# Rotary logits of a latent-KV attention as two single-pass split products in place of one float32 product

## The chip, the cores and the metric

One core of a Trainium2 chip runs the whole program, two transformer blocks for 512 tokens of width 1024. The metric is the device time in microseconds of one execution. Engines are named as the profile names them: PE (TensorE, matmuls), PEld (its weight loads), DVE (VectorE), ACT (ScalarE), POOL (GpSimd) and SP (the queue that issues most loads).

## The reference

The second block's last attention is the one that the change touches. Cut to what matters:

```python
def mla_attention(h, pos, w_dq, cq_norm, w_uq, q_nope_norm, q_pe_norm, w_o, k_nope, k_pe, v):
    c_q = rms_norm_2(h @ w_dq, cq_norm)
    q = (c_q @ w_uq).reshape(b, s, MLA_HEADS, MLA_QK_NOPE + MLA_QK_ROPE)   # 16 heads, 128 + 64
    q_nope = rms_norm_2(q[..., :MLA_QK_NOPE], q_nope_norm)
    q_pe = rotary(rms_norm_2(q[..., MLA_QK_NOPE:], q_pe_norm), pos)
    def block(args):                                                       # 4 blocks of 128 queries
        i, qn, qp = args
        sc = (jnp.einsum('bqhd,bkhd->bhqk', qn, k_nope)
              + jnp.einsum('bqhr,bkr->bhqk', qp, k_pe)).astype(jnp.float32) * scale
        sc = jnp.where(causal_mask(i, s), sc, NEG_INF)
        a = jax.nn.softmax(sc, axis=-1)
        return jnp.einsum('bhqk,bkhv->bqhv', a.astype(v.dtype), v)
```

Each head's logits are a product over 128 plain dimensions and one over 64 rotary dimensions. The rotary keys `k_pe` are shared by all heads.

## The kernel before

Everything is held transposed, features on the 128 partitions and the 512 tokens along the free dimension. The kernel is written as stages, each with one function per engine (`tensor`, `scalar`, `vector`); every engine runs its list of instructions in the order written, and semaphores tie the lists together. Large weight products are made of three passes of float32r data (`mm3`, L317 to L319): the weights and the activations are split into a rounded part and its rest (`w_hi`, `w_lo` by L291 and L300 on DVE), and high by high, high by low and low by high are added up in PSUM. The attention's own products (logits, transposes, values) are float32 matmuls; each of these shows as two instructions in the trace.

The stage `Latents` makes the compressed keys and queries and the rotary keys: `rotary_keys` (L2759 to L2769) leaves `kpe`, which has two versions: the keys in partitions 0 to 63 with zeros below, and the keys in 64 to 127 with zeros above. The zeros are two memsets at the start of the stage's `vector` (L2718, L2719).

The stage `Mla` follows. Its 16 heads are taken as 8 pairs, r from 0 to 7. One tile `qpe` holds both heads' rotary queries of a pair, head 0 in partitions 0 to 63 and head 1 in 64 to 127. A unit u is one head and one block b of 128 queries, so there are 8 units to a pair and 64 in all; block b has 128(b+1) keys. PE's list for unit u is: `logits(u)` (L3406 plain, L3407 rotary, L3408 the causal mask, bf16), the sums of squares (L3385) of what the unit before projected, the projections of the next pair (`mm3` passes or L3335 to L3337), `turn(u-2)` (transposes, L3416), `values(u-3)` (L3430). The projections are spread over units by the tables `EVEN` and `ODD`; `rotate` (L3392) turns the next pair's rotary queries into PSUM bank 7 at the end of unit 4 for an odd r and of unit 6 for an even r.

On DVE unit u is: `row_max(u)` (L3573), `normalize(u-1)` (L3579, L3582), at some units `output_lo` (L3588), `norm_out` of what was projected before (L3559), `round_both` of a weight slot (L291, L300), and last, at the same unit as `rotate`, `rope(r)` (L3562 to L3568): three instructions that end with the rotated queries in `qpe`. ACT has `exp(u)` (L3507), the norm's logarithm and exponential (L3495, L3499), the squares (L3479) and `turned_out` (L3515), which takes the transposed probabilities to `mpt`.

Three waits of PE look at `rope`: the sum of squares of K1 or Q1 waits for its first instruction (it frees bank 7), the first unit of a pair waits for its last, and so does, in `vector`, all that stands behind it on DVE.

Of the kernel before, what the change touches and what calls it, by code (L numbers as in the profile page):

```python
# [20 lines left out]
F32 = mybir.dt.float32  # L21
# [133 lines left out]
class Kernel:  # L155


    def __init__(self, nc, ctx, dram, V):
# [5 lines left out]
        def overlay(*groups):  # L164
# [4 lines left out]
            for n in [n for n in range(len(groups)) if n != widest] + [widest]:  # L169
# [43 lines left out]
            (self.cqh, self.cql, self.ckh, self.ckl, self.cos, self.sin, self.kpe, self.qpe, self.mq, self.mk,  # L213
# [37 lines left out]
             ("cos", [P, T], F32), ("sin", [P, T], F32), ("kpe", [P, 2, T], F32), ("qpe", [P, 2, T], F32),  # L251
# [11 lines left out]
        )  # L263
        self.ps = ctx.enter_context(nc.psum_tensor("ps", [P, 8, T], F32))
# [2254 lines left out]
class Latents(Stage):  # L2519
# [8 lines left out]
    def plan(self):  # L2528
        k = self.k
        self.w = k.slots(self.SIZES, 1)  # L2530
        self.e = k.events(1, gained_hi=range(2 * KD), gained_lo=range(2 * KD), square_summed=[0], log_ms=[0], rstd=[0],
                          evacuated=range(7), norm_sq=range(7), norm_sum=range(3), norm_log=range(3), norm_rstd=range(3),
                          scaled=range(6), x_hi=range(6), x_lo=range(6), norm_out=range(7), rope_rot=[0],
                          rope_step=range(19))
        self.positions_here = k.moved("positions_in")
        self.steps = 0
# [179 lines left out]
    def vector(self, dve):  # L2716
        k, V = self.k, self.k.V
        dve.memset(k.kpe[64:P, 0, :], 0.0).then_inc(k.sem["norm_out"], 1)  # L2718
        dve.memset(k.kpe[0:64, 1, :], 0.0).then_inc(k.sem["norm_out"], 1)  # L2719
# [39 lines left out]
    def rotary_keys(self, dve):  # L2759

        k = self.k
        plain = k.latk[:, 2, :]
        dve.wait_ge(*self.on("rope_step", 18))
        dve.tensor_tensor(k.sq[1][:], k.ps[:, 0, :], k.sin[:], ALU.mult).then_inc(k.sem["norm_out"], 1)
        dve.tensor_tensor(plain, plain, k.cos[:], ALU.mult).then_inc(k.sem["norm_out"], 1)
        dve.wait_ge(*self.on("norm_out", 4))
        for j in range(2):
            own = slice(64 * j, 64 * j + 64)
            dve.tensor_tensor(k.kpe[own, j, :], plain[own, :], k.sq[1][own, :], ALU.add).then_inc(k.sem["norm_out"], 1)  # L2769
# [476 lines left out]
class Mla(Stage):  # L3246
# [10 lines left out]
    ROT_UNIT = {True: 6, False: 4}  # L3257

# [4 lines left out]
    def plan(self):  # L3263
# [3 lines left out]
        for r in range(1, self.PAIRS):  # L3267
# [7 lines left out]
                     if key[1] == "V3" or key[1] == ("K1" if key[0] else "Q1")}  # L3275
# [4 lines left out]
                          rope_made=range(3 * self.PAIRS), logits=u, row_min=u, probs_raw=u, row_recip=u, probs=u,  # L3280
# [95 lines left out]
    def sum_squares(self, pe, r, name):  # L3376
# [4 lines left out]
        if name == {0: "K1", 1: "Q1"}[r % 2] and r:  # L3381
            pe.wait_ge(*self.on("rope_made", 3 * r))
# [5 lines left out]
    def rotate(self, pe, r, after):  # L3388
        k = self.k
        pe.wait_ge(*self.on("norm_out", self.normed[(r, "PE")]))  # L3390
        pe.wait_ge(*self.on("norm_log", self.normed[(r, after)]))
        pe.matmul(k.ps[:, 7, :], k.rot, k.qpe[:, r % 2, :], start=True, stop=True).then_inc(k.sem["rope_rot"], 1)  # L3392

    def logits(self, pe, u):
        k, r, j, b = self.k, u // 8, u // 4 % 2, u % 4
        if b == 0:
            pe.wait_ge(*self.on("norm_out", self.normed[(r, f"Q{j}")]))
            pe.wait_ge(*self.on("norm_out", self.normed[(r, f"K{j}")]))
            if j == 0:
                pe.wait_ge(*self.on("rope_made", 3 * r + 2))  # L3400
# [6 lines left out]
        pe.matmul(bank[:, 0:n], k.qpe[:, r % 2, b * P:n], k.kpe[:, j, 0:n], start=False, stop=False)  # L3407
# [146 lines left out]
    def norm_out(self, dve, r, name):  # L3554
        k, n, V = self.k, self.normed[(r, name)], self.k.V
        dst = k.qpe[:, r % 2, :] if name == "PE" else (k.mq if name[0] == "Q" else k.mk)[:, r % 2, int(name[1]), :]
# [5 lines left out]
    def rope(self, dve, r):  # L3562
        k, own = self.k, self.k.qpe[:, r % 2, :]
# [3 lines left out]
        dve.wait_ge(*self.on("rope_made", 3 * r + 1))  # L3567
        dve.tensor_tensor(own, own, k.rope[:], ALU.add).then_inc(k.sem["rope_made"], 1)  # L3568

# [436 lines left out]
```

## Time and profile before

| what | before |
|---|---|
| median of 3 runs (lowest to highest) | 3025.54 us (3025.52 to 3026.2) |
| profiled execution: span, first to last instruction | 3022.4 us |
| PE busy | 2902.0 us (96%) |
| DVE busy | 1803.7 us (60%) |
| ACT busy | 903.8 us (30%) |
| chain that ended last | PE 87%, DVE 7%, ACT 3%, issue 2% |
| mean granted clock of PE | 0.987 |
| DMA queues in the profile | two "hardware_dynamic", two "instruction" |

The profile gives no time of its own for the profiled execution beside its span; the median of the three runs is 3.1 us above it. The busy share of PE is a sum over matmuls whose ends are modelled, so it hides short stalls. What a stretch is worth has to be read from the chain of waits and from the order of instructions in time.

### The profile page before, as it was taken

The numbers are of one execution on the slowest core, as the hardware profiler recorded it, in microseconds if no ns is written. First come the engines' busy times: TensorE is split into PE (matmuls) and PEld (weight loads), VectorE is DVE, ScalarE is ACT, GpSimd is POOL, SyncE is SP. The second block draws the span as 40 slices with busy tenths as digits, with TensorE's granted clock in tenths as the row PEclk, the third lists the DMA queues.
The fourth block names the chain that finished last, engine by engine and source line by source line (L and its number), as shares of the span: only waits on it lengthen the run. The fifth ranks groups of instructions, "written<-read, shape, count | busy, mean of one in ns | idle before, by whom it ended". The sixth has DMA issues, their size and how long they took to land.

```text
span 3022.4 us, 36545 instructions
## 1 busy us (share of the span) xinstructions
PE 2902.0 (96%) x12794; PEld 2213.6 (73%) x12802; DVE 1803.7 (60%) x2790; ACT 903.8 (30%) x1606; POOL 294.4 (10%) x213
## 2 busy tenths in 40 slices
PE   8999989998998999998999899999889999999999
PEld 6777867776676888866766688887657768788887
DVE  6775356885445555356466777746655554777646
ACT  2111023343433111033255333302355540333202
POOL 1111003332140111000000011100000000011100
PEclk9999999999999999999999999999999999999999
DMA  4335322121122223322221222332211102222332
GB/s 150 109 109 122 104 75 79 63 70 56 49 78 70 90 97 94 96 68 87 86 77 66 77 90 97 97 93 82 87 42 36 36 29 91 82 92 97 97 93 96
DMA packets 78549, 249.86 MB, mean 83 GB/s; under 512 B 8840, under 2 KB 15368, under 8 KB 78440
## 3 DMA queue, kind: packets, MB, share of 16 engines
q1 hardware_dynamic: 65232, 229.74, 23.1%
q10 hardware_dynamic: 13208, 18.71, 2.4%
q8 instruction: 64, 1.05, 0.1%
q14 instruction: 45, 0.37, 0.0%
HBM read 238.32 MB, written 9.96 MB: 82 GB/s over the span
## 4 chain that ended last, share of the span: by engine, by line
PE 87%; DVE 7%; ACT 3%; issue 2%; DMA 0%; ACTq 0%; POOL 0%; SPq 0%; DVEq 0%; POOLq 0%
PE ps L317 24%; PE ps L318 24%; PE ps L319 24%; PE ps L3385 1%; PE ps L3430 1%; PE ps L3406 1%; PE ps L3407 1%; PE ps L906 1%; PE ps L2902 1%; DVE w_lo L300 1%; PE ps L2178 1%; DVE w_hi L291 1%; PE ps L2887 1%; PE ps L2157 1%; PE ps L1545 1%
## 5 line engine op out<-in xcount | busy, mean ns | idle before, releaser
L317 PE MATMUL ps<-xh,w_hi 128*128 128x512 f32 x2152 | 881.2, 409 | 40.6 <-DVE xl L487 13.3
L318 PE MATMUL ps<-xl,w_hi 128*128 128x512 f32 x2152 | 855.7, 398 | 0.0
L319 PE MATMUL ps<-xh,w_lo 128*128 128x512 f32 x2152 | 855.3, 397 | 0.0
L291 DVE CAST w_hi<-raw 128x1024 fp32r<-128x1024 f32 (+1 forms) x438 | 302.5, 691 | 736.2 <-PE ps L319 700.5
L317 PEld LDWEIGHTS ps<-xh,w_hi 128*128 128x128 f32 x2152 | 407.1, 189 | 185.4 <-issue 54.0
L300 DVE TENSOR_TENSOR w_lo<-raw,w_hi 128x1024 fp32r<-128x1024 f32 (+1 forms) x386 | 502.5, 1302 | 28.5
L319 PEld LDWEIGHTS ps<-xh,w_lo 128*128 128x128 f32 x2152 | 406.8, 189 | 100.0
L318 PEld LDWEIGHTS ps<-xl,w_hi 128*128 128x128 f32 x2152 | 407.9, 190 | 98.4 <-issue 7.2
L317 PE MATMUL ps<-ah,w_hi 128*128 128x512 f32 x704 | 278.1, 395 | 0.0
L318 PE MATMUL ps<-al,w_hi 128*128 128x512 f32 x704 | 278.1, 395 | 0.0
L319 PE MATMUL ps<-ah,w_lo 128*128 128x512 f32 x704 | 278.1, 395 | 0.0
L1104 POOL TENSOR_TENSOR al<-tmp,ah 128x512 f32 x44 | 65.0, 1478 | 1353.2 <-ACT ah L1079 1353.2
L310 POOL TENSOR_TENSOR w_lo<-raw,w_hi 128x512 fp32r<-128x512 f32 x104 | 146.8, 1432 | 444.6 <-DVE w_hi L291 444.6
L318 PEld LDWEIGHTS ps<-al,w_hi 128*128 128x128 f32 x704 | 132.0, 187 | 32.4
L317 PEld LDWEIGHTS ps<-ah,w_hi 128*128 128x128 f32 x704 | 132.0, 187 | 32.3
L319 PEld LDWEIGHTS ps<-ah,w_lo 128*128 128x128 f32 x704 | 131.9, 187 | 32.2
L1089 DVE SCALAR_TENSOR_TENSOR tmp<-ps,vecs,tmp 128x511 f32<-128x511 f32 (+1 forms) x176 | 131.1, 745 | 13.7 <-ACT tmp L1074 0.9
L1074 ACT ACTIVATE tmp<-ps,vecs 128x512 f32<-128x512 f32 x88 | 68.6, 780 | 181.1 <-PE ps L319 179.6
L850 POOL TENSOR_TENSOR al<-tmp,ah 128x512 f32 x44 | 57.5, 1306 | 534.4 <-ACT ah L790 534.4
L790 ACT ACTIVATE ah<-tmp 128x512 f32 (+1 forms) x44 | 27.9, 633 | 234.1 <-DVE tmp L828 234.1
L577 ACT ACTIVATE sq<-ps 128x512 f32<-128x512 f32 x24 | 14.4, 599 | 248.4 <-PE ps L319 248.4
L577 ACT ACTIVATE sq<-h 128x512 f32<-128x512 f32 x16 | 10.1, 632 | 218.8 <-DVE h L594 218.8
(429 smaller groups left out, 3707.8 us busy)
## 6 DMA issues: line engine op xcount, KB each, us to landing
raw<-in_ffn_up SPq DMA_DIRECT2D x90, 512.0 KB, 3.3
raw<-in_conv_up SPq DMA_DIRECT2D x88, 512.0 KB, 3.2
raw<-in_ffn_down SPq DMA_DIRECT2D x32, 512.0 KB, 3.6
raw<-in_conv_down SPq DMA_DIRECT2D x32, 512.0 KB, 3.5
raw<-in_merge SPq DMA_DIRECT2D x24, 512.0 KB, 3.2
raw<-in_ple_gate SPq DMA_DIRECT2D x24, 512.0 KB, 3.2
raw<-in_diff SPq DMA_DIRECT2D x24, 512.0 KB, 3.3
raw<-in_mla SPq DMA_DIRECT2D x20, 512.0 KB, 3.2
```

The costliest lines, as they stand in the source:

```text
L291: dve.tensor_copy(self.w_hi[s][:, 0:n], self.raw[r][:, 0:n]).then_inc(self.sem["slot_hi"], 1)
L300: dve.tensor_tensor(self.w_lo[s][:, 0:n], self.raw[r][:, 0:n], self.w_hi[s][:, 0:n].bitcast(F32), ALU.subtract).then_inc(self.sem["slot_sp ...
L310: ins = pool.tensor_tensor(self.w_lo[s][:, own], self.raw[r][:, own], self.w_hi[s][:, own].bitcast(F32), ALU.subtract)
L317: pe.matmul(out, wh, xh, start=start, stop=False)
L318: pe.matmul(out, wh, xl, start=False, stop=False)
L319: return pe.matmul(out, wl, xh, start=False, stop=stop)
L850: pool.tensor_tensor(k.al[:, 2 * i + pair, :], k.tmp[2 * pair][:], k.ah[:, 2 * i + pair, :].bitcast(F32), ALU.subtract).then_inc(k.sem["ac ...
L906: mm = pe.matmul(k.ps[32 * g:32 * g + 32, 4 + r, 0:n], k.bdiag[:], self.selected(b, g), start=True, stop=True)
L1074: act.activation(k.tmp[pos][:], k.ps[:, pos, :], ACT.Identity, bias=self.col(i, pos, 3), scale=self.col(i, pos, 2)).then_inc(k.sem["conv0" ...
L1089: dve.scalar_tensor_tensor(k.tmp[pos][:, back:T], k.ps[:, pos, 0:T - back], self.col(i, pos, 2 - back), k.tmp[pos][:, back:T], ALU.mult, A ...
L1104: pool.tensor_tensor(k.al[:, 2 * i + pair, :], k.tmp[2 * pair][:], k.ah[:, 2 * i + pair, :].bitcast(F32), ALU.subtract).then_inc(k.sem["ac ...
L1545: mm = pe.matmul(k.ps[:, 4 + l % 2, own], keys[:, own], queries[:, own], start=True, stop=True)
```

## The change

The rotary product is no longer one float32 matmul. The rotated queries of a head are split into a rounded part and its rest, both float32r, and stacked: for head 0 the rounded part in partitions 0 to 63 and the rest in 64 to 127, for head 1 the other way round (`qst`, two versions for consecutive pairs). The keys are held three times (`kst`): version 0 is the rounded keys in all 128 partitions, versions 1 and 2 are the rest of the keys in the half where that head's rounded queries lie, and zero in the other. Two float32r matmuls with the same stationary operand then give rounded by rounded plus rest by rounded, and rounded by rest. `rope` gets four more DVE instructions, each of 64 partitions by 512: two rounding copies and two subtractions, the latter writing to the other half of the partitions. `rotary_keys` gets two more. The zeros come from two copies of a constant in place of two memsets. `qpe` has one version in place of two. The new tile `qst` needs room, for which the scratch reserved for dynamic DMA descriptors is set to 8192 bytes.

```diff
-             ("cos", [P, T], F32), ("sin", [P, T], F32), ("kpe", [P, 2, T], F32), ("qpe", [P, 2, T], F32),
+             ("cos", [P, T], F32), ("sin", [P, T], F32), ("kst", [P, 3, T], R), ("qpe", [P, T], F32),
...
+        self.qst = sb("qst", [P, 2, 2, T], F32R)
...
     def vector(self, dve):
         k, V = self.k, self.k.V
-        dve.memset(k.kpe[64:P, 0, :], 0.0).then_inc(k.sem["norm_out"], 1)
-        dve.memset(k.kpe[0:64, 1, :], 0.0).then_inc(k.sem["norm_out"], 1)
+        for j in range(2):
+            rest = slice(64 - 64 * j, P - 64 * j)
+            none = k.half_ones[rest, 64 * j:64 * j + 64].unsqueeze(1).to_broadcast([64, T // 64, 64])
+            dve.tensor_copy(k.kst[rest, 1 + j, :].rearrange("p (a c) -> p a c", c=64), none
+                            ).then_inc(k.sem["norm_out"], 1)
...
         dve.wait_ge(*self.on("norm_out", 4))
+        dve.tensor_tensor(plain, plain, k.sq[1][:], ALU.add).then_inc(k.sem["norm_out"], 1)
+        dve.wait_ge(*self.on("norm_out", 5))
+        dve.tensor_copy(k.kst[:, 0, :], plain).then_inc(k.sem["norm_out"], 1)
+        dve.wait_ge(*self.on("norm_out", 6))
         for j in range(2):
             own = slice(64 * j, 64 * j + 64)
-            dve.tensor_tensor(k.kpe[own, j, :], plain[own, :], k.sq[1][own, :], ALU.add).then_inc(k.sem["norm_out"], 1)
+            dve.tensor_tensor(k.kst[own, 1 + j, :], plain[own, :], k.kst[own, 0, :].bitcast(F32), ALU.subtract
+                              ).then_inc(k.sem["norm_out"], 1)
...
             if j == 0:
-                pe.wait_ge(*self.on("rope_made", 3 * r + 2))
+                pe.wait_ge(*self.on("rope_made", self.ROPE * (r + 1) - 1))
...
         pe.matmul(bank[:, 0:n], k.mq[:, r % 2, j, b * P:n], k.mk[:, r % 2, j, 0:n], start=True, stop=False)
-        pe.matmul(bank[:, 0:n], k.qpe[:, r % 2, b * P:n], k.kpe[:, j, 0:n], start=False, stop=False)
+        rotary = k.qst[:, r % 2, j, b * P:n]
+        pe.matmul(bank[:, 0:n], rotary, k.kst[:, 0, 0:n], start=False, stop=False)
+        pe.matmul(bank[:, 0:n], rotary, k.kst[:, 1 + j, 0:n], start=False, stop=False)
...
     def rope(self, dve, r):
-        k, own = self.k, self.k.qpe[:, r % 2, :]
+        k, own, at = self.k, self.k.qpe[:], self.ROPE * r
...
-        dve.wait_ge(*self.on("rope_made", 3 * r + 1))
+        dve.wait_ge(*self.on("rope_made", at + 1))
         dve.tensor_tensor(own, own, k.rope[:], ALU.add).then_inc(k.sem["rope_made"], 1)
+        dve.wait_ge(*self.on("rope_made", at + 2))
+        head = [slice(64 * j, 64 * j + 64) for j in range(2)]
+        for j in range(2):
+            dve.tensor_copy(k.qst[head[j], r % 2, j, :], k.qpe[head[j], :]).then_inc(k.sem["rope_made"], 1)
+        for j in range(2):
+            dve.wait_ge(*self.on("rope_made", at + 3 + j))
+            dve.tensor_tensor(k.qst[head[1 - j], r % 2, j, :], k.qpe[head[j], :], k.qst[head[j], r % 2, j, :].bitcast(F32),
+                              ALU.subtract).then_inc(k.sem["rope_made"], 1)
...
-    nc = bacc.Bacc("TRN2", target_bir_lowering=False, num_devices=1)
+    nc = bacc.Bacc("TRN2", target_bir_lowering=False, num_devices=1, dynamic_dma_scratch_size=8192)
```

Two places show where the new instructions stand. Line numbers of the changed kernel are its own. The first place is DVE at the rope of pair 3, at unit 4 of pair 2. Before:

```order
L3582 TENSOR_SCALAR sq<-sq,small 128x512 [waits row_recip]
L3565 TENSOR_TENSOR rope<-ps,sin 128x512 [waits rope_rot]
L3566 TENSOR_TENSOR qpe<-qpe,cos 128x512
L3568 TENSOR_TENSOR qpe<-qpe,rope 128x512 [waits rope_made]
L3573 TENSOR_REDUCE small<-ps 128x1 [waits logits]
```

The same place in the changed kernel:

```order
L3602 TENSOR_SCALAR sq<-sq,small 128x512 [waits row_recip]
L3577 TENSOR_TENSOR rope<-ps,sin 128x512 [waits rope_rot]
L3578 TENSOR_TENSOR qpe<-qpe,cos 128x512
L3580 TENSOR_TENSOR qpe<-qpe,rope 128x512 [waits rope_made]
L3584 CAST qst<-qpe 64x512 [waits rope_made]
L3584 CAST qst<-qpe 64x512
L3587 TENSOR_TENSOR qst<-qpe,qst 64x512 [waits rope_made] x2
L3593 TENSOR_REDUCE small<-ps 128x1 [waits logits]
```

Two rounding copies and two subtractions now stand between the end of the rotation and the next unit's `row_max`.

The second place is PE at the end of pair 3, where the sum of squares of K1, a turn, a product with the values and the first logits of pair 4 follow each other. Before:

```order
L3406 MATMUL ps<-mk,mq 128x512 [waits probs_raw]
L3407 MATMUL ps<-kpe,qpe 128x512
L3408 MATMUL ps<-maskc 128x128
L3385 MATMUL ps<-tmp,consts 128x512 [waits rope_made,norm_log,norm_sq]
L3416 MATMUL ps<-consts,rs 128x128 [waits probs_t_out,probs]
L3416 MATMUL ps<-consts,rs 128x128
L3430 MATMUL ps<-mpt,mvr 128x128 [waits y_lo,probs_t_out]
L3406 MATMUL ps<-mk,mq 128x128 [waits rope_made,probs_raw,norm_out]
L3407 MATMUL ps<-kpe,qpe 128x128
L3408 MATMUL ps<-maskc 128x128
```

The same place in the changed kernel:

```order
L3416 MATMUL ps<-mk,mq 128x512 [waits probs_raw]
L3418 MATMUL ps<-kst,qst 128x512
L3419 MATMUL ps<-kst,qst 128x512
L3420 MATMUL ps<-maskc 128x128
L3395 MATMUL ps<-tmp,consts 128x512 [waits rope_made,norm_log,norm_sq]
L3428 MATMUL ps<-consts,rs 128x128 [waits probs_t_out,probs]
L3428 MATMUL ps<-consts,rs 128x128
L3442 MATMUL ps<-mpt,mvr 128x128 [waits y_lo,probs_t_out]
L3416 MATMUL ps<-mk,mq 128x128 [waits rope_made,probs_raw,norm_out]
L3418 MATMUL ps<-kst,qst 128x128
L3419 MATMUL ps<-kst,qst 128x128
L3420 MATMUL ps<-maskc 128x128
```

The order is unchanged but for one rotary matmul that is now two; the wait for `rope_made` at the first logits of a pair now stands for the last of seven rope instructions, not the last of three.

## Rows read from the trace of the kernel before

**Rows 1.** Stretches: us, PE, PEld, DVE, ACT, POOL busy (x), PEclk, DMA share, GB/s

```profile
2196.20:2240.50 44.30, 36.67 (x136) 24.05 (x135) 22.08 (x37) 24.92 (x46) 0.00 (x0) 0.92 0.14 48
2312.40:2384.20 71.80, 71.39 (x345) 51.23 (x345) 37.44 (x78) 37.90 (x86) 0.00 (x0) 1.00 0.11 37
```

**Rows 2.** Chain that ended last, PE's steps in one head: start us, us, what

```profile
2322.93 0.22 PE ps L3407 x2
...
2323.21 0.29 PE ps L3335
2323.49 0.23 PE ps L3336
...
2327.26 0.43 PE ps L3407 x2
...
2332.36 0.65 PE ps L3407 x2
...
2337.76 0.86 PE ps L3407 x2
```

**Rows 3.** Chain that ended last, from the rotation for pair 3

```profile
2312.42 0.69 DVE rope L3565
...
2314.44 0.34 DVE small L3573
...
2319.35 0.48 DVE small L3573
...
2321.67 0.27 ACT mpt L3515
...
2322.07 0.41 PE ps L3416 x2
```

**Rows 4.** Order in time, DVE in the rope of pair 3: start us, us, what [idle before]

```profile
2313.03 0.68 DVE L3566 TENSOR_TENSOR qpe<-qpe,cos 128x512 f32<-128x512 f32 x1
2313.74 0.69 DVE L3568 TENSOR_TENSOR qpe<-qpe,rope 128x512 f32<-128x512 f32 x1
2314.36 0.42 DVE L3573 TENSOR_REDUCE small<-ps 128x1 f32<-128x256 f32 x1
```

**Rows 5.** Order in time, DVE: nearest shapes to the new instructions

```profile
2141.77 0.43 DVE L291 CAST w_hi<-raw 128x512 fp32r<-128x512 f32 x1 [2.59 <-PE ps L319]
...
2199.70 1.41 DVE L2769 TENSOR_TENSOR kpe<-latk,sq 64x512 f32<-64x512 f32 x2
```

**Rows 6.** Order in time, DVE at the ropes of pairs 0 and 4

```profile
2220.59 0.69 DVE L3568 TENSOR_TENSOR qpe<-qpe,rope 128x512 f32<-128x512 f32 x1
2222.72 0.75 DVE L3559 SCALAR_TENSOR_TENSOR mq<-ps,vecs,tmp 128x512 f32<-128x512 f32 x1 [1.43 <-ACT tmp L3499]
...
2360.39 0.69 DVE L3568 TENSOR_TENSOR qpe<-qpe,rope 128x512 f32<-128x512 f32 x1
```

**Rows 7.** Order in time, PE at the first logits of pairs 0 and 4

```profile
2221.43 0.46 PE L3406 MATMUL ps<-mk,mq 128*128 128x128 f32 x2 [0.23 <-DVE qpe L3568]
...
2359.90 1.10 PE L3385 MATMUL ps<-tmp,consts 128*128 128x512 f32 x2
2360.83 0.38 PE L3416 MATMUL ps<-consts,rs 128*128 128x128 f32 x2
2361.05 0.39 PE L3430 MATMUL ps<-mpt,mvr 128*128 128x128 f32 x2
2361.34 0.46 PE L3406 MATMUL ps<-mk,mq 128*128 128x128 f32 x2
```

**Rows 8.** Order in time, PE at waits for the turned probabilities, last pair

```profile
2477.11 0.52 PE L3416 MATMUL ps<-consts,sq 128*128 128x128 f32 x3 [1.01 <-ACT mpt L3515]
```

**Rows 9.** Order in time, DVE behind the zeros and behind the rotary keys

```profile
2132.45 5.40 DVE L2702 SCALAR_TENSOR_TENSOR xl<-h,vecs,xh 128x512 fp32r<-128x512 f32 x8 [1.44 <-ACT xh L2610]
...
2205.76 0.75 DVE L3559 SCALAR_TENSOR_TENSOR mk<-ps,vecs,tmp 128x512 f32<-128x512 f32 x1 [4.65 <-ACT tmp L3499]
```

**Rows 10.** Order in time, PE after idle times elsewhere in the program

```profile
1339.30 0.50 PE L317 MATMUL ps<-xh,w_hi 128*128 128x512 f32 x1 [2.97 <-DVE xl L1330]
...
1340.50 0.63 PE L318 MATMUL ps<-xl,w_hi 128*128 128x512 f32 x1
...
1645.45 0.52 PE L2915 MATMUL ps<-consts,dw 128*128 128x128 f32 x3 [2.80 <-ACT dpt L2998]
```

More of the change, by code:

```diff
@@ L212, in __init__ @@
             (self.oh, self.ol, self.dq, self.dk, self.dvr, self.de, self.dw, self.dpt, self.dout, self.dbias),
-            (self.cqh, self.cql, self.ckh, self.ckl, self.cos, self.sin, self.kpe, self.qpe, self.mq, self.mk,
+            (self.cqh, self.cql, self.ckh, self.ckl, self.cos, self.sin, self.kst, self.qpe, self.mq, self.mk,
              self.mvr, self.mpt, self.rope, self.zh, self.zl),
@@ L2532, in plan @@
                           evacuated=range(7), norm_sq=range(7), norm_sum=range(3), norm_log=range(3), norm_rstd=range(3),
-                          scaled=range(6), x_hi=range(6), x_lo=range(6), norm_out=range(7), rope_rot=[0],
+                          scaled=range(6), x_hi=range(6), x_lo=range(6), norm_out=range(9), rope_rot=[0],
                           rope_step=range(19))
@@ L3257 @@
     ROT_UNIT = {True: 6, False: 4}
+    ROPE = 7
     def __init__(self, k, latents):
@@ L3279, in plan @@
                           norm_out=five, v_out=range(len(values)), rope_rot=range(self.PAIRS),
-                          rope_made=range(3 * self.PAIRS), logits=u, row_min=u, probs_raw=u, row_recip=u, probs=u,
+                          rope_made=range(self.ROPE * self.PAIRS), logits=u, row_min=u, probs_raw=u, row_recip=u, probs=u,
                           probs_t=u, probs_t_out=u, pv=u, y_hi=range(16), y_lo=range(16))
@@ L3381, in sum_squares @@
         if name == {0: "K1", 1: "Q1"}[r % 2] and r:
-            pe.wait_ge(*self.on("rope_made", 3 * r))
+            pe.wait_ge(*self.on("rope_made", self.ROPE * r))
         if (r, name) == (0, "Q1"):
@@ L3391, in rotate @@
         pe.wait_ge(*self.on("norm_log", self.normed[(r, after)]))
-        pe.matmul(k.ps[:, 7, :], k.rot, k.qpe[:, r % 2, :], start=True, stop=True).then_inc(k.sem["rope_rot"], 1)
+        pe.matmul(k.ps[:, 7, :], k.rot, k.qpe[:], start=True, stop=True).then_inc(k.sem["rope_rot"], 1)
     def logits(self, pe, u):
@@ L3555, in norm_out @@
         k, n, V = self.k, self.normed[(r, name)], self.k.V
-        dst = k.qpe[:, r % 2, :] if name == "PE" else (k.mq if name[0] == "Q" else k.mk)[:, r % 2, int(name[1]), :]
+        dst = k.qpe[:] if name == "PE" else (k.mq if name[0] == "Q" else k.mk)[:, r % 2, int(name[1]), :]
         gain = V["b_q_pe_norm" if name == "PE" else "b_q_nope_norm" if name[0] == "Q" else "k_nope_norm"]
```

## The prediction

> **What bounds the kernel now.** I first read the stretches of the last attention. In a period of two pairs of heads PE is busy 71.39 of 71.80 us, DVE 37.44 and ACT 37.90; only the start of the stage, before the second rope, has real holes, 36.67 of 44.30 us [rows 1]. By shares, PE is the bound and DVE is half idle, so PE's savings should count and DVE's additions be free. Busy shares are averages, so I read the chain next. It runs through PE almost everywhere, but at each rope of an odd pair it leaves PE when the rotation is done (2312.42) and comes back only at 2322.07: rope on DVE, the next unit's row maximum, its exponential and the norm on ACT, the weight rounding and another row maximum on DVE, the probabilities' way to `mpt`, then PE's transposes [rows 3]. In those 9.65 us PE works almost the whole time too, and is stopped for a few tenths only: two paths of nearly the same length. Last I read the order in time at the rope of an even pair. There PE's first logits of the new pair start at 2361.34; the product with the values before them began at 2361.05 and takes 0.22, so PE could have started at 2361.27. The rope's last instruction began at 2360.39 and took 0.69, so it ended at 2361.08 [rows 6, 7]. At pair 0 the same wait shows 0.15 from the rope's end (2220.59 + 0.69 = 2221.28) to PE's start at 2221.43. So the even rope is on time to within 0.1 us. There is no slack under `rope` anywhere, and the change makes `rope` longer.
>
> **The change, what PE gains.** The old rotary product takes PE 0.86, 0.65, 0.43 and 0.22 us for 512, 384, 256 and 128 keys [rows 2], 2.16 us for a head. A single-pass float32r matmul of 512 columns takes 0.23 [rows 2], and one that follows another kind takes up to 0.06 more (0.29 against 0.23); the first rotary matmul now follows a float32 one, so I charge 0.05 a unit. No row shows a float32r matmul narrower than 512. I scale the part above 0.02 with the width: 0.18, 0.13 and about 0.08 for 384, 256 and 128. The gains are then 0.86 - 0.47 - 0.05 = 0.34, 0.65 - 0.36 - 0.05 = 0.24, 0.43 - 0.25 - 0.05 = 0.13 and 0.22 - 0.16 - 0.05, about nothing. That is 0.71 us a head, 11.4 over 16 heads, if all of it lay on the path. The two ends: without the extra for switching and at the pure width, 0.9 to 1.0 a head; and, if a narrow float32r matmul costs as much as the float32 product of its width, 0.22 lost at each 128.
>
> The Trainium skill, "TensorE: Matmul & The Clock Gate", section "Back-to-back issue gap", puts a sustained matmul of N=128 at about 81 ns, weight load included. No run here shows it for float32r; it would keep the 128 case where I put it, and a float32 pass of 0.11 (half of 0.22) is above it.
>
> Not all of this counts. Where the path runs through DVE, PE's gain only makes PE wait longer. In a period of 16 units the path is on PE for these: after the odd rope's detour 256, 384, 512, 256, 384 (0.13 + 0.24 + 0.34 + 0.13 + 0.24 = 1.08), and after the even rope 256, 384, 512 (0.71). That is 1.79, three times 5.4. Before the first odd rope 0.24 + 0.34 = 0.58 count. Behind the last one are two heads with nothing beside them; there PE's wait of 1.01 at the transposes starts when the 512-key logits end [rows 8], so those move up in full, and the 128-key unit lies in the wait: 2 x 0.71 = 1.4. **Gain on the path: 7.4 us**; with the better prices 9.6, with the worse one about 5.
>
> **What DVE adds.** Four instructions of 64 x 512 behind the rope's addition. Partitions don't set DVE's time here: a 64 x 512 addition takes 1.41 / 2 = 0.70 from start to start, and a rounding copy of 512 columns 0.43 [rows 5]. An instruction starts 0.71 after the one that it waits for and 0.62 after one that it doesn't [rows 4], a difference of 0.09; so a copy that isn't waited for steps by some 0.37. The sum is 0.09 + 2 x 0.37 + 2 x 0.70 = 2.2 us. The bounds are 1.9 (subtractions at 0.6) and 2.9 (copies at 0.70 like the rest). No row shows a DVE write to other partitions than it reads; I take it as free, and the upper bound covers it.
>
> Where it falls. **Odd ropes (4):** what is queued behind on DVE is the row maximum of the next unit, and ACT's exponential waits for that, and the whole detour of rows 3 behind it. All links are serial, so the detour is 2.2 longer, and PE arrives 0.13 + 0.24 + 0.34 earlier at a wait that is later. 4 x 2.2 = 8.8. PE's stop is split in two, since the squares of K1 (ACT, behind the exponential) also come late: about 1.8 at their sum and 1.5 at the transposes. **Even ropes (3):** PE's first logits wait for the seventh instruction; DVE's row maximum behind it moves by as much, so the distances behind stay. 0.1 is lost to the slack: 3 x 2.1 = 6.3. **Pair 0:** the rope ends at 2221.28 + 2.2 = 2223.45, and the norm of Q1 behind it began at 2222.72, when ACT was ready [rows 6]; it starts 0.75 later, and the first row maximum, whose logits PE now begins at 2223.6, some 0.15 more: 0.9. **Lost on the path: 16.0 us.**
>
> The rest is hidden. The zeros: two copies of at most 0.70 in place of two memsets stand ahead of an instruction that sat 1.44 waiting for ACT. The rotary keys: two more instructions, 1.4 us at most, ahead of an idle time of 4.65 [rows 9]; were that cover gone, they would cost those 1.4. `qpe` in one version adds no wait: PE has read it before `rope` writes. The scratch for descriptors: the page lists no queue of software descriptors, so I give it nothing. DMA issues and SP's and POOL's lists are the same.
>
> **Sum:** 16.0 - 7.4 = 8.6 us more. The sum is made against the profiled span of 3022.4, which becomes 3031.0; the median of the runs is 3.1 above it, so 3025.5 + 8.6 = **3034.1 us**, 0.28% slower. With ends together, 7 x 1.9 + 0.6 - 9.6 = +4.3 and 7 x 2.9 + 1.6 - 5 = +17.
>
> **The rivals.** *(a) Covered.* PE is the bound and DVE's additions disappear under it: faster by 9.6 to 11.4 and more, about 3015. Decided at the even rope: it needs DVE's end at 2361.08 to be early, and rows 6 and 7 show it isn't. Only a rope whose four new instructions run far below 0.37 and 0.70 would do, or a large mistake in the rows read as serial. Chance 0.07. *(b) Only one kind of rope binds.* Say that the even ropes' 6.3 are absorbed because PE's gain there is smaller than I think or a wait runs in parallel: 8.8 + 0.9 - 7.4 = +2.3, or with the better prices 0: 3025 to 3028, no change. For it speaks that the even rope is not on the chain before; against it the 0.1 us. Chance 0.15. *(c) Narrow float32r is slow.* If 128 columns cost 0.22 each instead of 0.08, each such unit on the path loses 0.22 more than I have; about 10 to 12 of the 16 are there: +2.5, 3036.6. Nothing in the profile shows such a width, for or against. Chance 0.2. *(d) The clock.* Elsewhere a stop of 2.80 us left the matmuls behind it at their usual rate, and one of 2.97 was followed, a microsecond later, by float32r matmuls of 0.63, the rate of the 1.2 GHz level, where 0.40 is that of 2.4 GHz [rows 10]. At that level each 512-column matmul steps by about 0.2 more; half a dozen to a dozen of them make 1.5 to 2 us a time. My new stops are 1.5 to 2.4 us, below both, but at seven or eight places, and pair 0 has three close together. If half of them trip it, 4 x 1.7 = +7: 3041. Chance 0.1. The same page of the Trainium skill, section "Why this matters for your kernels", asks for no idle gaps above about 3 us between bursts of matmuls; by that rule the new stops would leave the clock alone, and the time would be my forecast's. The two waits in rows 10 agree with it. *(e) The split is not what it says*, for instance a product that stays in two instructions: the built order shows one instruction a matmul as for `mm3`, but the clock of the array decides. Then nothing is gained and 16 lost plus the second product, far above 3050. Chance 0.01.
>
> **How the numbers follow.** My forecast, with its own range of 3030 to 3038, has 0.47; (a) 0.07, (b) 0.15, (c) 0.2, (d) 0.1, (e) 0.01. Measurement tells this kernel from no change at about 0.2%, 6 us. Slower by more than that, above 3031.5: most of the forecast (0.37, since its ends with the better prices fall below), (c) 0.19, (d) 0.1, (e) 0.01, in all 0.67. Faster by more than that: 0.07 from (a), of which a part stays within, so 0.06. Within: 0.27. The range leaves out (a), (e) and the upper tail of (d), and takes in the half of (b) above 3027: 3027 to 3041.
>
> **What would show it.** Right: in the changed profile the four new instructions take 2.2 us from the end of the rope's addition to the next row maximum; PE's first logits of pairs 2, 4 and 6 wait for DVE (`qst`) about 2 us each; PE stops by 3 to 4 us in all behind each odd rope; the granted clock stays at 1.00 in the periods; a period is 74.3 us (71.8 + 2.2 + 2.1 - 1.8). Rotary matmuls step by 0.23, 0.18, 0.13, 0.08. Wrong: a period at or below 71.8 us, which would mean that the ropes' chains are not serial or that PE gains far more than 0.7 a head; a wait of PE for `kst` or for the start of Latents; or a clock below 1.00 in the periods.

## Result, and the profile after

| what | before | changed |
|---|---|---|
| median (lowest to highest, runs) | 3025.54 us (3023.08 to 3026.97, 5) | 3037.89 us (3035.2 to 3039.98, 5) |
| ratio to before, 95% interval | | 1.0041 (1.0029 to 1.0053) |
| profiled span | 3022.4 us | 3035.4 us |
| PE busy | 2902.0 us (96%) | 2894.0 us (95%) |
| DVE busy | 1803.7 us (60%) | 1822.8 us (60%) |
| mean granted clock of PE | 0.987 | 0.985 |

The change makes the kernel 12.4 us slower (0.41%), inside the range of 3027 to 3041 and 3.8 us above the forecast of 3034.1. A second comparison, on another occasion, gave 3038.5 us and 1.0044 (1.003 to 1.0057).

**Where it went.** The page of the changed kernel has the shares of the chain that ended last:

```profile
PE 85%; DVE 8%; ACT 3%; issue 2%; DMA 0%; ACTq 0%; POOL 0%; SPq 0%; DVEq 0%; POOLq 0%
```

PE's share of the chain fell by 2 points and DVE's rose by 1. The last attention, cut at the first rope instruction of pairs 1, 3, 5 and 7, shows where. The columns are those of [rows 1]; the changed kernel:

```profile
2203.60:2244.10 40.50, 36.71 (x131) 24.81 (x132) 19.62 (x36) 19.05 (x37) 0.00 (x0) 0.87 0.12 39
2244.10:2318.30 74.20, 68.19 (x345) 50.56 (x344) 42.01 (x86) 37.90 (x86) 0.00 (x0) 1.00 0.11 36
2318.30:2394.10 75.80, 69.78 (x345) 51.78 (x345) 42.02 (x86) 38.00 (x86) 0.00 (x0) 0.98 0.10 35
2394.10:2468.40 74.30, 68.29 (x346) 50.61 (x345) 42.06 (x86) 37.91 (x86) 0.00 (x0) 1.00 0.11 36
```

Before, PE was busy 71.39 of 71.80 us in such a period [rows 1]. Now it is busy 68.19 of 74.20 at the same clock: 3.2 us of work went, and 5.6 us of stops came. DVE has 42.0 us in place of 37.4, and still idles for 32 of 74. From the first sum of squares of the stage to a turn near its end, the same instructions in both kernels, it went like this (starts of instructions, us):

| stretch | before | changed | more |
|---|---|---|---|
| first sum of squares to rope of pair 1 | 38.28 | 40.48 (clock 0.87) | 2.20 |
| to rope of pair 3 | 71.88 | 74.25 (1.00) | 2.37 |
| to rope of pair 5 | 71.82 | 75.81 (0.98) | 3.99 |
| to rope of pair 7 | 71.83 | 74.29 (1.00) | 2.46 |
| to a turn in the last pair | 30.14 | 30.78 | 0.64 |
| sum | 283.95 | 295.61 | 11.66 |

The 11.66 stand in this stage. The other 1.34 of the 13.0 us between the spans lie ahead of it; behind it both have 536.2. Ahead of it the two profiles differ by the clock, at places that the change doesn't touch. The stop of 2.80 us of [rows 10] is one: before, the matmuls behind it ran at full rate, and in the changed kernel they don't:

```profile
1646.32 0.52 PE L2924 MATMUL ps<-consts,dw 128*128 128x128 f32 x3 [2.80 <-ACT dpt L3007]
...
1647.77 0.63 PE L320 MATMUL ps<-oh,w_lo 128*128 128x512 f32 x1
```

The kernel scratch, below, does what before does, and its clock falls there too; its span is 3021.3 for 3022.4. It is also the better partner for the start of the stage:

```profile
2201.80:2239.40 37.60, 34.58 (x130) 22.93 (x131) 17.27 (x30) 18.93 (x37) 0.00 (x0) 0.96 0.13 42
```

This start has 37.60 us with the clock at 0.96, where before's has 38.28 at 0.94. Up to the same turn scratch has 283.26 us, so against it the changed kernel's stage is 12.35 us longer, as much as the medians differ.

**The rope.** The order in time of DVE at the rope of pair 3 (start us, us, what; it answers to [rows 4]):

```profile
2319.66 0.69 DVE L3580 TENSOR_TENSOR qpe<-qpe,rope 128x512 f32<-128x512 f32 x1
2320.38 0.87 DVE L3584 CAST qst<-qpe 64x512 fp32r<-64x512 f32 x2
2321.29 1.40 DVE L3587 TENSOR_TENSOR qst<-qpe,qst 64x512 fp32r<-64x512 f32 x2
2322.62 0.41 DVE L3593 TENSOR_REDUCE small<-ps 128x1 f32<-128x256 f32 x1
```

From the start of the rope's addition to that of the row maximum behind it are 2.96 us, where [rows 4] had 2314.36 - 13.74 = 0.62. The four instructions cost 2.34 us. All four lie on the chain (start us, us, what):

```profile
2319.66 0.70 DVE qpe L3580
2320.38 0.42 DVE qst L3584
2320.83 0.43 DVE qst L3584
2321.29 0.69 DVE qst L3587
2322.01 0.69 DVE qst L3587
2322.69 0.34 DVE small L3593
...
2327.60 0.48 DVE small L3593
...
2330.32 0.41 PE ps L3428 x2
...
2369.64 0.70 DVE qst L3587
2370.34 0.25 issue
2370.59 0.46 PE ps L3416 x2
```

The detour of [rows 3], from the rotation's end to PE's transposes, took 9.65 us and takes 2330.32 - 2318.33 = 11.99: 2.34 more, link by link. The last three steps are new: at the even rope the chain also goes from DVE to PE's first logits, where before it stayed on PE:

```profile
2361.21 0.22 PE ps L3430 x2
2361.44 0.36 PE ps L3406 x2
```

PE in order of time, behind the odd rope of pair 3 and before the first logits of pairs 2 and 4 (the brackets are idle time before the row and what ended it):

```profile
2296.33 0.46 PE L3416 MATMUL ps<-mk,mq 128*128 128x128 f32 x2 [2.24 <-DVE qst L3587]
...
2297.16 0.40 PE L319 MATMUL ps<-cql,w_hi 128*128 128x512 f32 x1
...
2325.49 1.12 PE L3395 MATMUL ps<-tmp,consts 128*128 128x512 f32 x2 [1.65 <-ACT tmp L3491]
...
2330.32 0.41 PE L3428 MATMUL ps<-consts,sq 128*128 128x128 f32 x2 [1.31 <-ACT mpt L3527]
...
2366.80 1.10 PE L3395 MATMUL ps<-tmp,consts 128*128 128x512 f32 x2 [0.48 <-DVE rope L3577]
...
2370.59 0.46 PE L3416 MATMUL ps<-mk,mq 128*128 128x128 f32 x2 [2.24 <-DVE qst L3587]
...
2371.76 0.63 PE L319 MATMUL ps<-cql,w_hi 128*128 128x512 f32 x1
```

The stops of a period, 1.65 + 1.31 at the odd rope and 0.48 + 2.24 at the even one, add up to 5.68 us, the 5.6 from above. The last rows hold what I had given a chance of 0.1 only. Behind the stop of pair 4 the 512-column matmul of L319 takes 0.63, the rate of the 1.2 GHz level, and behind a stop just as long at pair 2 it takes 0.40, that of 2.4 GHz. The period with pair 4 has clock 0.98 and is 75.81 - 74.25 = 1.56 us longer.

**The rotary products.** PE at the logits of 512, of 128 and of 256 keys:

```profile
2327.46 1.02 PE L3416 MATMUL ps<-mk,mq 128*128 128x512 f32 x2
2327.92 0.79 PE L3418 MATMUL ps<-kst,qst 128*128 128x512 f32 x1
2328.55 0.39 PE L3419 MATMUL ps<-kst,qst 128*128 128x512 f32 x1
2328.78 0.23 PE L3420 MATMUL ps<-maskc 128*128 128x128 bf16 x1
...
2330.79 0.39 PE L3416 MATMUL ps<-mk,mq 128*128 128x128 f32 x2
2330.93 0.31 PE L3418 MATMUL ps<-kst,qst 128*128 128x128 f32 x1
2331.07 0.27 PE L3419 MATMUL ps<-kst,qst 128*128 128x128 f32 x1
2331.19 0.23 PE L3420 MATMUL ps<-maskc 128*128 128x128 bf16 x1
...
2334.88 0.60 PE L3416 MATMUL ps<-mk,mq 128*128 128x256 f32 x2
...
2335.55 0.23 PE L3420 MATMUL ps<-maskc 128*128 128x128 bf16 x1
```

Read the starts here: the durations of matmuls in flight overlap. From the logits' first row to the mask are 1.32 us at 512 keys, 0.67 at 256 and 0.40 at 128; 384 keys have 1.00. Before they were 1.71, 0.87, 0.45 and 1.29. So the gain is 0.39, 0.29, 0.19 and 0.05 us for 512, 384, 256 and 128 keys, or 0.92 us a head. The second product steps by 0.23, 0.18, 0.12 and 0.12.

**The rest** is hidden, as said. The instructions behind the zeros and behind the rotary keys on DVE answer to [rows 9]:

```profile
2134.84 2.74 DVE L2703 SCALAR_TENSOR_TENSOR xl<-h,vecs,xh 128x512 fp32r<-128x512 f32 x4 [1.82 <-ACT xh L2611]
...
2206.99 0.75 DVE L3571 SCALAR_TENSOR_TENSOR mk<-ps,vecs,tmp 128x512 f32<-128x512 f32 x1 [3.36 <-ACT tmp L3511]
```

Behind the zeros (two copies, 0.88 us together) DVE still waits 1.82 us for ACT, and behind the keys 3.36 in place of 4.65.

### The profile page after: what moved, and what is told of

Its sections match the earlier page's. It is cut to its first block, busy times and chain, and to the rows that moved or that the text cites. A ratio compares the mean times of both kernels' runs of the same rounds, so it can differ in the third digit from the quotient of the medians.

```text
span 3035.4 us, 36579 instructions
## 1 busy us (share of the span) xinstructions
PE 2894.0 (95%) x12794; PEld 2216.3 (73%) x12802; DVE 1822.8 (60%) x2824; ACT 904.1 (30%) x1606; POOL 293.9 (10%) x213
## 4 chain that ended last, share of the span: by engine, by line
PE 85%; DVE 8%; ACT 3%; issue 2%; DMA 0%; ACTq 0%; POOL 0%; SPq 0%; DVEq 0%; POOLq 0%
PE ps L318 24%; PE ps L319 24%; PE ps L320 24%; PE ps L3442 1%; PE ps L3395 1%; PE ps L3416 1%; DVE w_lo L301 1%; PE ps L2911 1%; PE ps L907 1%; DVE w_hi L292 1%; PE ps L2179 1%; PE ps L2896 1%; PE ps L2158 1%; PE ps L1546 1%; PE ps L2937 1%
## 5 line engine op out<-in xcount | busy, mean ns | idle before, releaser
L319 PE MATMUL ps<-xl,w_hi 128*128 128x512 f32 x2152 | 856.0, 398 | 0.0
L319 PEld LDWEIGHTS ps<-xl,w_hi 128*128 128x128 f32 x2152 | 408.2, 190 | 98.1 <-issue 7.2
L319 PE MATMUL ps<-al,w_hi 128*128 128x512 f32 x704 | 278.2, 395 | 0.0
L319 PEld LDWEIGHTS ps<-al,w_hi 128*128 128x128 f32 x704 | 132.0, 188 | 32.2
L578 ACT ACTIVATE sq<-h 128x512 f32<-128x512 f32 x16 | 10.1, 632 | 218.8 <-DVE h L595 218.8
```

Source lines behind the costliest of these rows:

```text
L319: pe.matmul(out, wh, xl, start=False, stop=False)
```

## Experiments

The theory: DVE's four instructions bind at both kinds of rope (some +16 us), PE's cheaper products give back about half, and some clock is lost at the stops. The rivals: the cost is not DVE's place but its amount, or only one kind of rope binds; the new scratch or the tile moves something; the clock makes most of it. Each kernel was timed in five rounds beside the kernel before. The first four share one set of runs of before (3024.79 us), the next four another (3025.41), the last two a third (3024.66).

**dve_only: the added DVE work without PE's gain.** The rotary product of before stays and reads `qpe` and `kpe` as before. `rope` also makes the split, which nobody reads, and PE waits for the seventh instruction. An excerpt of the edit, against the changed kernel:

```diff
-        rotary = k.qst[:, r % 2, j, b * P:n]
-        pe.matmul(bank[:, 0:n], rotary, k.kst[:, 0, 0:n], start=False, stop=False)
-        pe.matmul(bank[:, 0:n], rotary, k.kst[:, 1 + j, 0:n], start=False, stop=False)
+        pe.matmul(bank[:, 0:n], k.qpe[:, r % 2, b * P:n], k.kpe[:, j, 0:n], start=False, stop=False)
```

> The kernel before with the four splitting instructions added to each rope and the first logits of a pair waiting for the last of them, while the rotary product stays the float32 one (the new tile is written and never used). Serial ropes (my theory): each rope's path is 2.3 us longer by the changed kernel's trace, 4 x 2.3 + 3 x 2.2 + 0.9 = 16.7 us, so 3042 at full clock, and up to 3 us more if PE's clock falls behind the first rope as it did in the changed kernel. Rival, the additions are covered and the changed kernel's 12 us come from the matmuls: 0 to 2 us more, 3026 to 3028. Rival, only the odd ropes bind: 4 x 2.3 + 0.9 = 10, 3036.

Measured: 3046.41 us, ratio 1.007 (1.0056 to 1.0083), +21.6. Two periods of its profile:

```profile
2243.30:2319.90 76.60, 71.83 (x347) 51.30 (x345) 42.04 (x87) 37.91 (x86) 0.00 (x0) 1.00 0.11 35
2319.90:2398.00 78.10, 73.35 (x346) 52.42 (x345) 42.06 (x87) 38.04 (x86) 0.00 (x0) 0.98 0.10 34
```

At full clock a period has 76.53 us from rope to rope, 4.68 above the 71.85 of before: twice 2.34, so both kinds of rope bind, each with the whole of its four instructions. That rules out the rival by which only one kind binds. The time is 5 us above the 16.7 that were expected at full clock, since the clock fell at pair 0, in the second and in the third period (1.5 us each) and in the last pair. Without these falls the added work costs some 17.5 us, an estimate from the runs here: 7 x 2.34 = 16.4 at the later ropes and 1.1 at pair 0, where the start of the stage is 0.67 us shorter than in scratch in pe_only and 0.41 longer in filled.

**pe_only: PE's part without the added DVE work.** `rope` writes one rounded tile in its third instruction. This kernel leaves out the rests of the queries and mixes the two heads' rotary rows, so only its time says something:

```diff
-    ROPE = 7
+    ROPE = 3
...
-        rotary = k.qst[:, r % 2, j, b * P:n]
+        rotary = k.qst[:, r % 2, 0, b * P:n]
...
+        dve.tensor_tensor(k.qst[:, r % 2, 0, :], own, k.rope[:], ALU.add).then_inc(k.sem["rope_made"], 1)
```

> The changed kernel with the splitting left out: the rope's last addition writes the stacked tile directly, so the rests of the queries are left out and each head's product also takes in the other head's rows. PE's instructions and their shapes are those of the changed kernel, DVE's ropes are as long as before. My theory: the two single-pass products save 0.05, 0.13, 0.30 and 0.39 us at 128, 256, 384 and 512 keys (read from the changed kernel's trace), 0.87 a head, of which the parts outside the two detours of a period count: 3 x 2.2 + 0.7 + 1.6 = 9 us less, 3016.5. If everything counted it would be 16 x 0.87 = 14 us, 3011.5. Rival, the matmuls are no cheaper on the path: 3025.

Measured: 3014.73 us, ratio 0.9968 (0.9956 to 0.998), -10.1. One period:

```profile
2238.90:2308.50 69.60, 67.95 (x346) 50.53 (x345) 37.41 (x78) 37.90 (x86) 0.00 (x0) 1.00 0.12 39
```

A period is 69.59, 2.26 less than before. The prediction had put 1.79 of gain on the path. PE's busy time falls by more than the period, 3.44 us, so here too some of the gain only waits. (The 0.13 for 256 keys in the expectation is a misreading of the changed kernel's trace, which has 0.19.)

**defer_odd: the split behind the two row maxima that the odd detour needs.** For odd pairs the copies run in unit 5 and the subtractions in unit 6; the pair's first logits come four units after the rope:

```diff
+            if r < self.PAIRS and r % 2 and at == 5:
+                self.rounded(dve, r)
+            if r < self.PAIRS and r % 2 and at == 6:
+                self.rests(dve, r)
...
                     self.rope(dve, r)
+                    if r % 2 == 0:
+                        self.rounded(dve, r)
+                        self.rests(dve, r)
```

> The changed kernel, but the splitting of the odd pairs is taken out of the rope: the two copies follow the normalization in the next unit, the two subtractions that in the unit after, where DVE sat idle for about 1.5 us each. Serial ropes: the four odd detours go back to their old length, 4 x 2.3 = 9.2 us less than the changed kernel at the same clock, 3028 to 3029. Rival, DVE's amount of work matters and not its place: no change, 3037. Rival, only the even ropes' wait matters: no change either.

Measured: 3026.75 us, ratio 1.0007 (0.9998 to 1.0016): no difference from before that can be told, and some 10 to 11 below the changed kernel. Its second period:

```profile
2316.00:2387.90 71.90, 68.01 (x346) 50.50 (x345) 41.84 (x87) 37.92 (x86) 0.00 (x0) 1.00 0.11 37
```

DVE has the same 41.8 us of work, and the period is 71.9 in place of 74.25. At the odd rope the cost is the place of the four instructions, not their amount. The first period has 73.5 us with the clock at 0.98, behind the 2.24 us that PE still stops at the even rope.

**early_even: the even rope one step earlier on DVE.** The rounding of K1's weights, which stood ahead of it, goes behind it, to unit 7:

```diff
+            if r < self.PAIRS and r % 2 == 0 and at == 7:
+                k.round_both(dve, self.w, 0, at_slot + 2)
+                at_slot += 1
...
-                    if name in ("V3", "PE", "K1"):
+                    if name in ("V3", "PE", "K1") and (r % 2, at) != (0, 6):
```

> The changed kernel, but at the even ropes the rounding of a weight slot (1.9 us) that stood before the rope is moved behind it, into the next unit. The rope can then start when the rotation is done, about 1.2 us earlier, so each even rope's wait should shrink by 1.2 and the three by 3.6: 3034 to 3035 against the changed kernel's 3038, and PE's wait at the first logits of pairs 2, 4 and 6 falls from 2.24 to about 1.0. Rival, the slot's rounding comes too late for PE: a wait of the projection for DVE w_lo and no gain.

Measured: 3035.52 us, ratio 1.0037 (1.0023 to 1.0051), 10.7 above before, where the changed kernel is 12.4 and 13.8 above. The intervals overlap, so in the time a gain is small if it is there, and the clock was against it in every period. One period, and PE at the first logits of pair 4:

```profile
2316.90:2391.70 74.80, 69.57 (x345) 51.66 (x344) 42.03 (x86) 38.05 (x86) 0.00 (x0) 0.98 0.10 36
```

```profile
2368.17 0.46 PE L3416 MATMUL ps<-mk,mq 128*128 128x128 f32 x2 [1.91 <-DVE qst L3594]
...
2369.11 0.63 PE L319 MATMUL ps<-cql,w_hi 128*128 128x512 f32 x1
```

The wait of about 1.0 that was expected was a miss. The rope does come 0.95 us sooner: it begins 46.69 us behind the odd rope, where the changed kernel has 47.64. But the stop of 0.48 ahead went too, so PE came sooner to a wait that shrank only to 1.92. The clock fell behind that stop in three periods of three (74.84 each), though it is shorter than the 2.24 that left it alone in two of three. Less the 1.56 of a fall a period would have 73.3 us, so in this profile the falls take back what the earlier rope gives: the stage has 295.75 us for the changed kernel's 295.61.

**scratch: the kernel before with the descriptor scratch alone.**

```diff
-    nc = bacc.Bacc("TRN2", target_bir_lowering=False, num_devices=1)
+    nc = bacc.Bacc("TRN2", target_bir_lowering=False, num_devices=1, dynamic_dma_scratch_size=8192)
```

> The kernel before with nothing changed but the scratch for dynamic DMA descriptors, 8192 bytes in place of the default. My theory: no queue of the profile uses it, so no change, 3024.8 within 2. Rival, it slows DMA issue or moves tiles so that something is slower: 3027 or more, and then part of the changed kernel's 12 us is not the ropes'.

Measured: 3025.49 us, ratio 1.0003 (0.9993 to 1.0012), periods of 71.79 to 71.88. It costs nothing.

**filled: two matmuls in the even stops.** Once its PSUM bank is free, PE runs two float32 matmuls of constants before it waits for `rope`, for even pairs; their result is overwritten by the logits:

```diff
             if j == 0:
+                if u >= 2:
+                    pe.wait_ge(*self.on("probs_raw", u - 2))
+                if r % 2 == 0:
+                    for n in range(2):
+                        pe.matmul(k.ps[:, 0, :], k.ident, k.consts[:, 0:T], start=True, stop=True)
```

> The changed kernel with two float32 matmuls of constants (128 x 512 each, 1.7 us, the result is overwritten) put before PE's wait for the rope at the first logits of pairs 0, 2, 4 and 6, where PE stops for 2.2 to 2.6 us. Clock theory: those stops let the granted clock fall to 1.2 GHz, always at pair 0 and at one to three of the other places, 1.6 us each; filled, they don't, the stretches behind show a clock of 1.00 and a period is 74.2 us each time: 3 to 4 us less than the changed kernel, 3034. Rival, the falls come from the two stops behind the odd ropes or from elsewhere: unchanged, 3037. If the two matmuls are too long for a stop: 0.1 to 0.3 us more a place.

Measured: 3032.42 us, ratio 1.0025 (1.0016 to 1.0034). A period:

```profile
2315.40:2389.50 74.10, 69.99 (x349) 51.18 (x348) 42.04 (x86) 37.89 (x86) 0.00 (x0) 1.00 0.11 36
```

All three periods are at clock 1.00 and have 74.09 to 74.11 us. Work that does nothing makes the changed kernel 5.5 us faster. The stops behind the odd ropes are still there (1.67 and 1.31), so they aren't what lowers the clock. From the first sum of squares to the same turn are 291.10 us: 7.8 more than in scratch, which has the same 0.96 at the start, where the changed kernel has 12.35. Of these 4.5 us the clock takes 4.0: 1.56 in the period of pair 4 and 40.48 - 38.01 = 2.47 at the start of the stage, where the filled kernel has 0.96 for 0.87. The other 0.5 are 0.15 to 0.2 in each period, also where both clocks are 1.00: at the even ropes PE starts 0.06 us after DVE's last instruction, for 0.26 in the changed kernel. So at full clock the change itself costs 12.35 - 4.03 = 8.3 us.

**after_again and filled_again: the changed kernel and the filled one once more, side by side.**

> The changed kernel once more, beside the next run on the same chip. Clock theory: at least one stretch from pair 0 to the last pair has a granted clock below that of the kernel before, and it is not the same set of ropes as in the first profile, since the fall hangs on when a stop comes and not on its length alone; 3036 to 3039, 3 to 5 us above the run with PE's stops filled. Rival, the clock falls at fixed places: the same stretches as in the first profile (pair 0 and pair 4's first logits).

> The run with PE's stops at the even ropes filled by two matmuls of constants, once more, so that the two are compared on one chip. Clock theory: clock 1.00 in all periods of two pairs, 74.1 us each, 3032 to 3034. Rival, the first profile of it was a lucky one: periods of 75.7 among them, and the same time as the changed kernel.

Measured: 3038.5 us, 1.0044 (1.003 to 1.0057), and 3032.57 us, 1.0028 (1.0017 to 1.0038). The intervals do not quite part, but both pairs of medians differ by 5.5 to 5.9 us the same way, and in this second pair the slowest filled run (3034.53) is below the fastest of the changed kernel (3035.28). The changed kernel's profile now has two of three periods at 0.98, one of them this:

```profile
2241.90:2317.70 75.80, 69.75 (x345) 51.71 (x344) 42.06 (x86) 38.05 (x86) 0.00 (x0) 0.98 0.11 35
```

They have 75.83 and 75.84 us, and the third 74.28. The filled kernel again has three of 74.10 to 74.13.

**both: the split taken apart by heads, and the even rotation earlier.** Each head waits for its own half only. Head 0's half stays behind an even rope and goes to unit 5 for an odd one, head 1's half goes to unit 1 of the pair, or to unit 6 for an odd one. PE issues the even rotation ahead of `turn` and `values`, and the rounding moves as in early_even:

```diff
-            if j == 0:
-                pe.wait_ge(*self.on("rope_made", self.ROPE * (r + 1) - 1))
+            pe.wait_ge(*self.on("rope_made", self.ROPE * r + 4 + 2 * j))
...
+            if r < self.PAIRS and r % 2 == 0 and at == 6:
+                self.rotate(pe, r, "Q1")
             if u >= 2:
                 self.turn(pe, u - 2)
...
+            if at == 1:
+                if u // 8 == 0 or u // 8 % 2 == 0:
+                    self.split(dve, u // 8, 1)
+            if r < self.PAIRS and r % 2 and at in (5, 6):
+                self.split(dve, r, at - 5)
```

> The changed kernel with the splitting placed where DVE sat idle: odd pairs as in the run with deferred splitting, but one head a unit; at even ropes the weight slot's rounding behind the rope, the rotation ahead of the turns, head 0's split alone before the first logits and head 1's in the second unit of the pair. Serial ropes: no stop of more than 0.3 us at the even ropes, a period of 69.6 us as with the matmuls' part alone, so 3015 to 3017, 8 to 10 less than the kernel before. Rival, DVE's work as such costs time: 3025 or more.

Measured: 3016.25 us, ratio 0.9969 (0.9957 to 0.9981). A period:

```profile
2242.10:2311.50 69.40, 67.93 (x345) 50.50 (x345) 41.77 (x86) 38.01 (x86) 0.00 (x0) 1.00 0.12 39
```

The stops left in a period are 0.86 us at the odd rope's transposes and two below 0.3. The changed kernel's PE gain is there with all four instructions kept and out of the way: the period is that of pe_only to 0.2 us, and the sign is turned.

**spread: as both, and the odd rope's own second and third instruction moved too.** Only the multiplication that reads PSUM stays at unit 4; the other two go to unit 5, head 0's half to unit 6 and head 1's to unit 1:

```diff
         dve.tensor_tensor(k.rope[:], k.ps[:, 7, :], k.sin[:], ALU.mult).then_inc(k.sem["rope_made"], 1)
+
+    def spin(self, dve, r):
+        k, own, at = self.k, self.k.qpe[:], self.ROPE * r
         dve.tensor_tensor(own, own, k.cos[:], ALU.mult).then_inc(k.sem["rope_made"], 1)
...
+            if at == 1:
+                self.split(dve, u // 8, 1)
+            if r < self.PAIRS and r % 2 and at == 5:
+                self.spin(dve, r)
+            if r < self.PAIRS and r % 2 and at == 6:
+                self.split(dve, r, 0)
```

> As the run before it, and at the odd ropes only the first instruction of the rope (which frees the PSUM bank) stays ahead of the next unit's row maximum; the other two follow the normalization of that unit, the splits later still. The odd detour of DVE and ACT is then 1.3 us shorter than ever, and PE's remaining stop of 0.84 at its end goes: a period of 68.7 us, 3 x 0.85 + 0.85 = 3.4 us less than the run before it, 3012 to 3013. Rival, PE is stopped by something else at that place: as the run before it.

Measured: 3012.81 us (3010.51 to 3013.22), ratio 0.9955 (0.9942 to 0.9969), the fastest of all: 12.6 below before and 25 below the changed kernel. A period, then DVE at the rope of pair 3:

```profile
2241.60:2310.10 68.50, 67.90 (x346) 50.45 (x345) 41.85 (x86) 38.24 (x86) 0.00 (x0) 1.00 0.12 39
```

```profile
2310.14 0.69 DVE L3578 TENSOR_TENSOR rope<-ps,sin 128x512 f32<-128x512 f32 x1 [1.90 <-PE ps L3402]
2310.87 0.42 DVE L3598 TENSOR_REDUCE small<-ps 128x1 f32<-128x256 f32 x1
...
2311.61 0.68 DVE L3582 TENSOR_TENSOR qpe<-qpe,cos 128x512 f32<-128x512 f32 x1
2312.32 0.69 DVE L3584 TENSOR_TENSOR qpe<-qpe,rope 128x512 f32<-128x512 f32 x1
```

The row maximum now follows the first instruction of the rope by 0.73, where before two more stood between. PE's stop at the transposes is gone, the chain leaves PE at the odd rope for only 0.86 us (2310.11 to 2310.97) in place of 9.65, and PE has 67.90 of 68.50 us busy: it is the bound again.

## Why the prediction was right, and where it was off

- **DVE's additions bind at both ropes: right.** The steps are 2.34 for 2.2, so the four odd ropes cost 9.4. dve_only has 4.68 a period, where 2.2 + 2.1 = 4.3 was said, so the three even ones cost 7.0. The term was short by 0.14 a rope: a copy steps by 0.45 and a subtraction by 0.72 from start to start. Writing to other partitions cost nothing extra: 0.69 like the rest. The 0.1 us of slack at the even rope wasn't there either. In the changed kernel and in dve_only PE's first logits of such a pair start 0.26 us after DVE's last instruction, not 0.15 as at pair 0, and 2361.08 + 0.26 = 2361.34 is where they started before. The waits came where they were said: 2.24 at the even ropes for "about 2", 1.65 and 1.31 behind the odd ones for 1.8 and 1.5, so 2.96 in all for "3 to 4". The 0.48 at the sum of squares of K1, ahead of the even rope, was not forecast; it is PE arriving earlier at the rope's first instruction, and pe_only has it too.
- **PE's gain: too small.** 0.71 a head was said, 0.92 measured. The term that failed is the charge of 0.05 a unit for changing from float32 to float32r: without it the forecast's own widths give 0.39, 0.29, 0.18 and 0.06, where 0.39, 0.29, 0.19 and 0.05 were measured. On the path of a period, three units of 256, three of 384 and two of 512 keys make 2.22 in place of 1.79, and pe_only has 2.26. On the whole path 7.4 was said, and pe_only's stage is 9.1 us shorter than that of scratch.
- **The period** at full clock is 74.25 to 74.29 for 74.3. That closeness is luck: two errors offset each other, 4.68 - 2.26 by the runs and 4.3 - 1.8 by the forecast.
- **The sum** at full clock is 8.3 us by the runs, 8.6 by the forecast, and this is luck in the same way: some 17.5 lost for 16.0, and 9.1 gained for 7.4. Three periods at 2.4 make 7.3 and the tail 0.64; the start of the stage has 38.01 in the filled kernel for 37.60 in scratch, both with the clock at 0.96, so 0.4, where 0.9 - 0.58 = 0.3 was said.
- **Rival (d), the clock, had too small a chance.** "The granted clock stays at 1.00" was wrong in one period of three in one profile and in two of three in the other, and at pair 0 in both. The price of 1.7 a time was right (1.56). The mistake was the step "below both": it took 2.80 us without a fall as a length that is safe, from one row. That same stop, which the change doesn't touch, is followed by a fall in 8 of the 12 profiles of this case, scratch and the changed kernel among them. So the forecast held 8.6 and no clock, the difference is 12.4 of which 4.0 are the clock, and it came out 3.8 too low. The 3037.9 is at the upper edge of the forecast's own range of 3030 to 3038, and the second comparison's 3038.5 is beyond it: the time lies in the stated range because that reached on to 3041 for such a fall.
- **Rival (a)** asked for slack at the even rope that wasn't there; (b) falls with dve_only; (c) falls with the rows of 128 columns; (e) with the count of one instruction a matmul and the steps of 0.23.
- What stays open is what decides whether a stop of 2 us costs the clock. The same stop of 2.24 us, with the same work around it, was followed by a fall at pair 4 in one profile and at pairs 2 and 4 in the other.

## What to carry to other kernels

Before work is moved from the bound engine to one that is half idle, look at where it lands in that engine's list: here four cheap DVE instructions, in one place that PE waits for twice a period, cost some 17 us. Most of that work a unit or two later, with the rotation earlier, cost next to nothing and turned 12 us lost into 13 us gained. A producer's last instruction need not be what its first consumer waits for: let each head wait for its own half, and let the row maximum that another engine's chain hangs on go first. When PE waits, read the matmuls behind the stop as well, since a stop can cost more than its length.

## What the runs showed of the hardware

- **The clock falls behind stops shorter than 3 us, but not always.** Granted clock and matmul durations (0.63 for 0.40) show a fall to the 1.2 GHz level behind stops of 2.24 us at the even ropes (3 of 6 in the two profiles of the changed kernel, 2 of 3 in dve_only, 1 of 3 in defer_odd), 1.92 us (3 of 3 in early_even) and 2.6 us at pair 0 (5 of 5 profiles that have it). The stop of 2.80 us in [rows 10] had none before, and one in 8 of all 12 profiles. In the last pair there was one at 1.17 us in dve_only and at 1.21 us in both, each with another stop of 0.9 us shortly ahead. Each fall in a period costs 1.5 to 1.6 us more than the stop itself. The Trainium skill, "TensorE: Matmul & The Clock Gate", section "Why this matters for your kernels", advises against idle gaps above about 3 us; these runs don't agree with that as a bound, since gaps well below it were followed by a fall.
- **Idle work can pay.** Two float32 matmuls of 512 columns in each even stop kept the clock at 1.00 in six periods of six and gave back 5.5 to 5.9 us.
- **Narrow float32r matmuls of one pass are cheap**: the second product steps by 0.23, 0.18, 0.12 and 0.12 us at 512, 384, 256 and 128 columns, and the pair of them takes 0.46, 0.35, 0.24 and 0.18, against 0.86, 0.65, 0.43 and 0.22 for one float32 product [rows 2]. The Trainium skill, "TensorE: Matmul & The Clock Gate", section "Back-to-back issue gap", puts a sustained N=128 at about 81 ns. Here the step at 128 columns was longer, 0.12, with another float32r product ahead and a bf16 one behind.
- **DVE at half the partitions takes as long as at all**: 0.42 for a rounding copy of 64 x 512, where one of 128 x 512 has 0.43 [rows 5], and 0.69 for a subtraction, where an addition of 128 x 512 has 0.69 [rows 4], also where it writes to the other half.
